# Seven block products for the down projections of two FFN chunks, with x moved through three tiles and the low parts of weight blocks shared between VectorE and GpSimd

## The reference

```python
def swiglu(h, w_gu, w_d):
    gu = h @ w_gu
    g, u = gu[..., :D_FF], gu[..., D_FF:]
    return (jax.nn.silu(g) * u) @ w_d
...
hh = modulate(x, norm_g[l, 0], mod[:, 0], mod[:, 1])
x = x + 0.5 * mod[:, 2, None] * swiglu(hh, ffn_w_gu[l, 0], ffn_w_d[l, 0])
```

## Time and profile before

| what | value |
|---|---|
| median of 3 runs | 2325.98 us |
| the runs | 2325.94 to 2327.22 us |
| the profiled execution, own time | 2325.12 us |
| its span | 2323.3 us |
| granted TensorE clock | 0.99 of full |

### The profile page before, as it was taken

One profiled execution on the slowest core, in us unless ns is written; L12 is line 12 of the kernel. 1 busy time (PEld: TensorE's weight loads), 2 busy tenths in 40 slices (PEclk: granted clock), 3 DMA queues, 4 the chain that ended last, 5 costly groups with the idle time before them and its releaser, 6 DMA issues.

```text
span 2323.3 us, 42586 instructions
## 1 busy us (share of the span) xinstructions
PE 2229.3 (96%) x17538; PEld 2093.0 (90%) x17538; DVE 1505.5 (65%) x2615; ACT 1004.6 (43%) x1673; POOL 173.7 (7%) x133
## 2 busy tenths in 40 slices
PE   5999999999999999999999999999799899999998
PEld 4999999999999999999999999999544499999997
DVE  5585748587657766666457757667466555858585
ACT  4342424367453434345353424345344534434252
POOL 0100101000000101010000101010000101001010
PEclk9999999999999999999999999999899999999999
DMA  7334334512423434333533333335699641322222
GB/s 321 128 127 164 123 114 152 180 42 100 148 91 117 161 123 143 138 128 111 210 126 112 125 128 123 123 107 211 215 361 407 233 146 50 104 102 82 83 94 74
DMA packets 77234, 338.41 MB, mean 146 GB/s; under 512 B 9458, under 2 KB 13682, under 8 KB 60914
## 3 DMA queue, kind: packets, MB, share of 16 engines
q1 hardware_dynamic: 73810, 330.83, 39.9%
q10 hardware_dynamic: 3232, 4.87, 0.6%
HBM read 328.44 MB, written 7.23 MB: 144 GB/s over the span
## 4 chain that ended last, share of the span: by engine, by line
PE 84%; DVE 8%; ACT 4%; issue 2%; DMA 1%; POOL 0%; SPq 0%; ACTq 0%; DVEq 0%; POOLq 0%
PE ps L616 21%; PE ps L697 12%; PE ps L700 12%; PE ps L699 11%; PE ps L618 11%; PE ps L626 3%; PE ps L628 3%; PE ps L627 3%; PE ps L586 2%; DVE w_lo L1694 1%; PE ps L942 1%; DMA ada_pro<-in_ada_w 1%; PE ps L974 1%; DVE xc L2131 1%; PE ps L961 1%
## 5 line engine op out<-in xcount | busy, mean ns | idle before, releaser
L697 PE MATMUL ps<-bx,w_hi 128*128 128x288 f32 x2016 | 597.1, 296 | 0.0
L700 PE MATMUL ps<-bx,w_lo 128*128 128x288 f32 x2016 | 595.2, 295 | 0.0
L699 PE MATMUL ps<-bx,w_hi 128*128 128x288 f32 x2016 | 593.9, 295 | 0.0
L616 PE MATMUL ps<-hn_hi,w_hi 128*128 128x288 f32 x1360 | 381.5, 295 | 2.6 <-POOL hn_lo L2380 2.3
L697 PEld LDWEIGHTS ps<-bx,w_hi 128*128 128x128 f32 x2016 | 378.5, 188 | 5.8 <-issue 5.3
L616 PE MATMUL ps<-hn_lo,w_hi 128*128 128x288 f32 x1360 | 380.1, 295 | 0.0
L700 PEld LDWEIGHTS ps<-bx,w_lo 128*128 128x128 f32 x2016 | 379.7, 188 | 0.0
L699 PEld LDWEIGHTS ps<-bx,w_hi 128*128 128x128 f32 x2016 | 379.7, 188 | 0.0
L618 PE MATMUL ps<-hn_hi,w_lo 128*128 128x288 f32 x1360 | 292.2, 296 | 0.0
L1694 DVE TENSOR_TENSOR w_lo<-raw,w_hi 128x1536 fp32r<-128x1536 f32 (+2 forms) x108 | 205.9, 1907 | 111.7 <-ACT w_hi L1061 93.7
L616 PEld LDWEIGHTS ps<-hn_hi,w_hi 128*128 128x128 f32 x1360 | 255.4, 188 | 7.4 <-issue 4.2
(11 more groups left out here) (293 smaller groups left out, 4084.6 us busy)
## 6 DMA issues: line engine op xcount, KB each, us to landing
raw<-in_w_gu SPq DMA_DIRECT2D x88, 1024.0 KB, 4.9
ada<-in_ada_w SPq DMA_DIRECT2D x120, 512.0 KB, 7.4
raw<-in_w_d SPq DMA_DIRECT2D x48, 768.0 KB, 4.2
kr<-in_k_cache SPq DMA_DIRECT2D x64, 512.0 KB, 7.1
vr<-in_v_cache SPq DMA_DIRECT2D x60, 512.0 KB, 12.1
ada_pro<-in_ada_w SPq DMA_DIRECT2D x8, 1024.0 KB, 18.4
raw<-in_w_d SPq DMA_DIRECT2D x16, 512.0 KB, 3.6
ada_early<-in_ada_w SPq DMA_DIRECT2D x16, 512.0 KB, 10.7
```

The lines of the kernel that those rows point to most:

```text
L616: pe.matmul(ps[:, 2 * s + n, 0:TH], whi, rhs(k, n)[r], start=(k == 0 and r == 0), stop=False)
L697: pe.matmul(out, whi[:, cols], high, start=(fresh and k == 0), stop=False, skip_group_check=not fresh)
L699: pe.matmul(out, whi[:, cols], low, start=False, stop=False, skip_group_check=not fresh)
L700: mm = pe.matmul(out, wlo[:, cols], high, start=False, stop=(k == 3), skip_group_check=not fresh)
```

## The change

The down stages of the second and third chunk become units of seven products too, of three tiles of depth: 7 x 3 x 3 = 63 matmuls. `seven_unit` replaces `fast_unit`, and the up and down units from the second chunk's first to the fourth chunk's last up unit form one chain. For this:

- **Turned tiles.** The up units of chunks two and three make, beside g * u, sums for t1, t2, t3 (in `tb`) and t4 (in `hn_hi`, `hn_lo`): VectorE does one sum of 288 columns a unit in product_first and two more in product_second of the last three; ScalarE makes high parts, VectorE the low parts of t2 and t4, GpSimd those of t1 and t3.
- **Low parts of weight blocks.** In up units on VectorE as before. For down units, GpSimd makes those of A11 (but not for the second down unit of a chunk), A22, A12 and S34, of 384 and 768 columns; VectorE makes S12. The order on each engine is written out below. GpSimd's low part of g * u has 288 columns in the first three up units and 576 in the last three.
- **x.** `tb` lies over x tiles 3 to 7 and the late constants. In the chain x has three places (`x_of`): ScalarE's queue stores tiles 3 to 7 to yT at its first unit; after each down unit it stores two tiles and fetches two. SyncE fetches the whole x and the late constants in the fourth chunk's up stage (`x_back`).
- **Results.** The residual of a down unit comes in three parts: row2 (second tile, after the unit), c11 and c12 (first tile, within it).
- The order and the waits of the constants' loads at the start are changed, and semaphores are merged.

The core of the diff:

```diff
+                if starts_chain(s):
+                    for i, v in enumerate(chain_of(s)):
+                        seven_unit(v, i == 0)
...
+                    for k in range(kh):
+                        high, low = seven_at(v, i, k)
...
+                if v["down"] == 0:
+                    pe.wait_ge(sems["turned_lo"], 2 * q + 1)
                 product(1, fresh=True).then_inc(sems["f_prod"], 1)
                 pe.wait_ge(sems["f_seed"], f + 1)
+                if v["down"] == 0:
+                    pe.wait_ge(sems["t_lo"], LOWS * s["ffn"] + 4 + 5 * (q % 2) + 3)
                 product(2).then_inc(sems["f_prod"], 1)
```

ScalarE, in the loop over the chain:

```diff
+                        if down == 0:
+                            turn_high("t2", "t2", 2, 1, SUMS * s["ffn"] + 12 * (q % 2) + 4 + 11)
+                        if before is not None and before["up"] is not None:
+                            fast_high(before)
...
+                        if after_down:
+                            x_store(before, 0)
...
+                        if i == 0:
+                            act.dma_start(yT[3:KT].rearrange("k p t -> p k t"), x[:, 3:KT, :]).then_inc(sems["x_out"], 16)
+                        if after_down:
+                            x_store(before, 1)
+                        if after:
                             high_a22(u + 1, f + 1, False)
                             high_s12(u + 1, f + 1, False)
+                        if turned is not None and up == 3:
+                            turn_high("t1", "t2", 0, 3, SUMS * s["ffn"] + 12 * (q % 2) + 4 + 3)
+                        if turned is not None and up == 5:
+                            turn_high("t2", "t2", 0, 2, SUMS * s["ffn"] + 12 * (q % 2) + 4 + 8)
+                            turn_high("t3", "t3", 0, 2, SUMS * s["ffn"] + 12 * (q % 2) + 4 + 8)
+                            turn_high("t4", "t4", 0, 2, SUMS * s["ffn"] + 12 * (q % 2) + 4 + 9)
```

VectorE:

```diff
+                    def residual_row2(v):
+
+                        st, k, u = v["s"], 2 * v["down"] + 1, v["u"]
+                        x_ready(v, 1)
+                        dve.wait_ge(sems["w_done"], u + 1 + CREDITS["w_done"])
+                        add_scaled(st, k, slice(0, TH), ps[:, 2 if u % 2 else 0, 0:TH])
+                        dve.wait_ge(sems["f_c22"], v["f"] + 1)
+                        add_scaled(st, k, slice(TH, SEQ), c22[:, 0:PB])
+                        dve.wait_ge(sems["s0_free"], u + 1 + CREDITS["s0_free"])
+                        add_samples(st, k, c22[:, PB:TH], st["res"], "s1_free")
...
+                        if before is not None and before["up"] is not None:
+                            product_first(before)
+                        if before is not None and before["down"] is not None:
+                            residual_row2(before)
...
+                        if up is not None:
+                            low_s34(u, f)
+                        if down == 0:
+                            turn_low("t2", 2, 1, HIGHS * s["ffn"] + 7 * (q % 2) + 4 + 5)
+                        if after:
                             sums_123(u + 1, f + 1)
...
+                            if not down:
+                                low_a11(u + 1, f + 1)
+                        if down == 0:
+                            turn_low("t3", 2, 1, HIGHS * s["ffn"] + 7 * (q % 2) + 4 + 6)
                         dve.wait_ge(sems["f_prod"], 5 * f + 3)
                         dve.wait_ge(sems["f_p5"], f + 1)
                         dve.tensor_tensor(ps[:, 3, 0:TH], ps[:, bank, 0:TH], p5, ALU.add).then_inc(sems["f_u4"], 1)
...
+                        if after and after["up"] is not None:
                             low_a22(u + 1, f + 1)
...
+                        if after:
+                            low_s12(u + 1, f + 1)
+                        if v["s"]["turned"] is not None and up == 5:
+                            turn_low("t2", 0, 2, HIGHS * s["ffn"] + 7 * (q % 2) + 4 + 2)
+                            turn_low("t4", 0, 2, HIGHS * s["ffn"] + 7 * (q % 2) + 4 + 4)
+                        if down == 0:
+                            turn_low("t4", 2, 1, HIGHS * s["ffn"] + 7 * (q % 2) + 4 + 7)
+                        if down is not None:
+                            residual_c11(v)
```

GpSimd:

```diff
+                        if down is not None:
+                            low_s34(u, f)
+                        if before is not None and before["up"] is not None:
+                            product_low(before)
...
+                        if after and down:
+                            low_quarter("a11", 0, 0, 0, u + 1, f + 1)
...
+                        if after and after["down"] is not None:
+                            low_quarter("a22", 6, 1, 1, u + 1, f + 1)
+                        if turned is not None and up == 3:
+                            turn_low("t1", "t2", 0, 3, HIGHS * s["ffn"] + 7 * (q % 2) + 4 + 1)
+                        if turned is not None and up == 5:
+                            turn_low("t3", "t3", 0, 2, HIGHS * s["ffn"] + 7 * (q % 2) + 4 + 3)
+                        if after and after["down"] is not None:
+                            low_quarter("a12", 3, 0, 1, u + 1, f + 1)
```

More of the change, by code:

```diff
@@ L145, in ffn @@
         for c, tiles in enumerate(CHUNKS):
-            stage("fast" if c else "up", tiles, src=w_gu[2 * layer + which], row=first)
+            stage("fast" if c else "up", tiles, src=w_gu[2 * layer + which], row=first,
+                  turned=c - 1 if c in (1, 2) else None)
             count["h"] += tiles
             count["fast"] += tiles if c else 0
+            count["ups"] += tiles if c else 0
             first += tiles
@@ L180, in trunk, with chain_of, starts_chain @@
             width[s["u"] + m] = 256 * s.get("k", KT)
-    fast_of = {s["u"] + m: s["fast"] + m for s in plan if s["kind"] == "fast" for m in range(s["units"])}
+    sevens = [s for s in plan if s["kind"] == "fast" or s.get("seven")]
+    fast_of = {s["u"] + m: s["fast"] + m for s in sevens for m in range(s["units"])}
+    half_tiles = {s["u"] + m: 4 if s["kind"] == "fast" else 3 for s in sevens for m in range(s["units"])}
+    def chain_of(s):
+        units = []
+        for t in plan[plan.index(s):]:
+            if t not in sevens:
+                break
+            for m in range(t["units"]):
+                up = t["kind"] == "fast"
+                units.append({"u": t["u"] + m, "f": t["fast"] + m, "up": m if up else None,
+                              "down": None if up else m, "s": t})
+        return units
+    def starts_chain(s):
+        return s["kind"] == "fast" and s["row"] == CHUNKS[0]
     u_out = next(s["u"] + s["units"] for s in plan if s["kind"] == "rglru")
@@ L884, in _ @@
                                  freed="hq_free" if s["kind"] == "q" and m == s["units"] - 1 else None)
-                if s["kind"] == "fast":
-                    for m in range(s["units"]):
-                        fast_unit(u0 + m, s["fast"] + m, m == 0)
-                if s["kind"] == "down":
+                if starts_chain(s):
+                    for i, v in enumerate(chain_of(s)):
+                        seven_unit(v, i == 0)
+                if s["kind"] == "down" and not s.get("seven"):
                     h_all = s["h"]
@@ L1327, in _ @@
                     high_s34(u0, s["fast"], True)
                     high_a22(u0, s["fast"], True)
-                    for m in range(s["units"]):
-                        u, f, more = u0 + m, s["fast"] + m, m + 1 < s["units"]
-                        bank = 2 if u % 2 else 0
-                        if m:
-                            fast_high(m - 1)
+                    for i, v in enumerate(chain):
+                        u, f, up, down = v["u"], v["f"], v["up"], v["down"]
+                        before, after = chain[i - 1] if i else None, chain[i + 1] if i + 1 < len(chain) else None
+                        turned = v["s"]["turned"]
+                        q = 2 * s["ffn"] + (turned or 0)
+                        bank = 2 if u % 2 else 0
+                        after_down = before is not None and before["down"] is not None
+                        if down == 0:
+                            turn_high("t2", "t2", 2, 1, SUMS * s["ffn"] + 12 * (q % 2) + 4 + 11)
+                        if before is not None and before["up"] is not None:
+                            fast_high(before)
@@ L1353, in _ @@
                             split_unit(((u + 1) // 2, u + 1), 0)
+                        if after_down:
+                            done = 8 * before["s"]["turned"] + 2 * before["down"] + 2
+                            for n in (done + 1, done + 2):
+                                if n < 16:
+                                    x_load(s["ffn"], n, done)
                         act.wait_ge(sems["out0_full"], u + 1)
[L1355 to L1356 removed]
+                        if up is not None:
+                            act.activation(gate2, ps[:, 3, 0:TH], ACT.Silu).then_inc(sems["s0_free"], 1)
```

(17 more changed lines are left out.)

387 lines of the change are left out of this document (277 added, 110 removed).

## The result

The changed kernel takes 2450.45 us (2444.94 to 2453.78, 4 runs), the kernel before 2325.96: 1.0532 times as long, 95% interval 1.0509 to 1.0554. I had said 2367 and a range up to 2392: the direction was right, the size a third of what came, and the time lies outside the range.

What follows compares the result with a forecast made beforehand. TensorE's order of work bounds the kernel before; the shared GpSimd/VectorE port would delay the changed units. Unit delays 51.6, cover -12.2 and x 2 sum to +41.4 on 2325.1: 2366.5, rounded to 2367 us, range 2306 to 2392.

Steps and rivals of the forecast that it cites:

- The bound of the kernel before, and the prices: Whole kernel: TensorE sets the time, 0.3 us slack before the fifth product; GpSimd's 384 columns priced at 1.01 us.
- What the change removes: 32 down units: 288 matmuls, 38.2 us off TensorE; a unit can then take 8.35 us at least.
- The down unit, 10.0: Later down units: GpSimd's low parts hold up VectorE, fifth product 1.66 us late, 10.0 us against 9.5.
- the rival in which such steps are held: Rival: VectorE's PSUM steps are held too, or the x store is late; 2390 to 2400, chance 0.06.
- a median near 1.4 for the sums of 384 columns: Sign in the down units' VectorE sums: median near 1.4 us instead of 0.55.
- Part cover: Rival: one low part misses the sums, 0.9 off each of 24 units; 2345 to 2326, chances 0.09 slower, 0.07 near 2326.
- The first down unit, 11.4 and the fifth up unit, +0.8: Each chunk: first down unit 11.4 us against 9.5 (+1.9); fifth up unit's fifth product 0.8 us late.
- The sixth up unit: Each chunk's last up unit: A22, t3, A12 on GpSimd, t2, t4 on VectorE; +2.25 us.
- The up units, "+0" for the first four: Up units one to four: an added VectorE sum offset by GpSimd's smaller low part, +0 us.
- x through three places, 2 us: Five-tile x store 0.5 us late per FFN, 2 in all; fetched x tiles land in units before their use.
- Cover, -12.2: Modulation parts on TensorE ahead of eight units let VectorE's work get on: 12.2 us saved.
- the rival with full cover: Rival: GpSimd's work is wholly covered; pure 2287, 2303 with half of some delays left; full or nearly full cover, chance 0.20.

Runs made afterwards that it cites:

- the doubled low part: Kernel before the change, with GpSimd making each product's low part twice in the fast units: 2386.84 us, ratio 1.0264.
- 2387.22: Changed kernel with product_second moved back behind low A12 and sum_4 in the up units: 2387.22 us, ratio 1.0262.
- 2391.02: Kernel before the change, with only product_second moved ahead of low A12 and sum_4: 2391.02 us, ratio 1.0274.
- 2417.77: Changed kernel without the stores and loads of x inside the chain (part of x wrong): 2417.77 us, ratio 1.0398.
- 2352.76: Changed kernel with product_second back and x in transit left out (part of x wrong): 2352.76 us, ratio 1.0111.
- 2377.39: Changed kernel with product_second back and the down units' low parts on VectorE: 2377.39 us, ratio 1.0218.
- 2321.84: Changed kernel with product_second back, down units' low parts on VectorE, x in transit left out (part of x wrong): 2321.84 us, ratio 0.9982.

## Why the prediction was wrong

**The bound of the kernel before, and the prices.** Right. TensorE set the time, and the slack before the fifth product was as small as read: the doubled low part, 1.1 us more on VectorE, made a unit 0.92 longer, so 0.2 of the 0.3 was there. GpSimd's 384 columns, where nothing holds them, take 1.00 to 1.01, as the slope had it.

**What the change removes.** Right in size, 38 us of matmuls. A down unit came to 8.35 only where a modulation part stood ahead of it, as the third one of the first FFN in the changed kernel. Even with x out and VectorE doing all of it, the down units of the fourth FFN take 8.75, 8.5 and 9.6 and the first 10.3.

**The down unit, 10.0.** Right in length, 9.86 and 9.78, but not by the port alone. The timeline of the second down unit of the changed kernel, VectorE, GpSimd, ScalarE; its first product starts at 2175.39:

```profile
2176.03 1.58 DVE L2222 SCALAR_TENSOR_TENSOR x<-sg,mod_g,x 128x224 f32<-128x224 f32 x1
...
2178.51 1.25 DVE L1865 TENSOR_TENSOR scratch<-scratch,raw 128x384 f32<-128x384 f32 x1
2179.68 1.37 DVE L1866 TENSOR_TENSOR raw<-raw 128x384 f32<-128x384 f32 x1
2180.98 0.45 DVE L2292 TENSOR_TENSOR ps<-ps,sg 128x288 f32<-128x288 f32 x1
```
```profile
2175.48 1.87 POOL L2672 TENSOR_TENSOR w_lo<-raw,w_hi 128x768 fp32r<-128x768 f32 x1 [2.58 <-ACT w_hi L1191]
2177.91 2.74 POOL L2665 TENSOR_TENSOR w_lo<-raw,w_hi 128x384 fp32r<-128x384 f32 x2 [0.55 <-ACT w_hi L1167]
```
```profile
2176.80 0.34 ACTq L1428 DMA_DIRECT2D out_yT<-x  x1
2177.24 0.53 ACT L1167 ACTIVATE w_hi<-raw 128x384 fp32r<-128x384 f32 x1
```

The residual's second step was stopped by low S34 (1.58 instead of 0.44), two of three sums by low A11 and A22 (1.25 and 1.37 instead of 0.55). The add ended 6.04 after the unit's first product began, where I had 6.4; TensorE stood 1.25 before the fifth product, where I had 1.66. The residual's first step, which reads PSUM, took its 0.52, so the rival in which such steps are held (the third of the four, not the last) is out. That is the lock that the Trainium skill describes (SBUF — State Buffer, "SBUF: two separate sides"), and here too the trace agrees with it, on both sides: which operations stop and that they stop for the whole of the other.

I had said a median near 1.4 for the sums of 384 columns. In the changed kernel the medians of the three are 1.59, 1.26 and 0.55, and 50 of the 96 sums were stopped; with product_second back and x out it is 28 of 96, and most take 0.55. The down units there show why the port alone is cheaper: second and third ones with no modulation part beside them took 9.1 to 9.4 in eight of twelve cases and 9.8 to 10.0 in four. That is the rival *Part cover*. In the units compared here a store of x tips it. Its issue on ScalarE (L1428) stands ahead of the high part of A11 (L1167), which starts 0.45 behind the seed instead of 0.30; low A11 on GpSimd starts 2.52 after the first product instead of 2.36. Then it misses the residual's last step, and it and low A22 fall among the sums. The prediction's "the two stores and two loads of x a unit lie in gaps of over 1 us" did not hold there. This is read from the timelines and was not tried by itself, and the four long units have no store, so other small delays do the same. That the down units came near 10.0 in the changed kernel is in part luck: with product_second back and no x, the three later down units of a chunk of the fourth FFN cost nothing in sum, where I had 1.5.

**The first down unit, 11.4 and the fifth up unit, +0.8.** Near enough once the order is back: 11.15 and 11.92 (11.80 and 13.32 in the changed kernel). The sixth up unit was over-priced, +2.25 against +1.8.

**The up units, "+0" for the first four and nothing for the fourth chunk.** This is the first step that failed. I priced what was added and left the moved product_second out. It is worth 63 us, shown from both sides (2387.22 and 2391.02), and 65 with x out (2417.77 less 2352.76).

**x through three places, 2 us.** The second step that failed: "the x tiles fetched ... land in units before their use" was written with no row behind it. A tile's place is free when its store has landed, 4.4 us in the median, and the load takes 3.1 more, and longer beside 2 MB of modulation weights; a down unit takes 9.9. It is worth 33 to 34 us with GpSimd's low parts, and 56 with faster down units (2377.39 less 2321.84). The other term here, 2 us for the store of five tiles, was nothing: the first up units of the second chunks are as long as before once the order is back.

**Cover, -12.2.** Right, but hidden in the changed kernel, where the chains of the four FFNs are 30.5, 30.7, 27.9 and 28.4 us longer than before: those with modulation parts lost as much as the fourth. With product_second back and x out they are 4.0, 5.3, 4.1 and 8.6 longer, so the three FFNs with parts lost 12.4 less than three like the fourth would have. The parts cover VectorE's work, but the weights that come for them made x late; moving those loads gave 16 us.

Put together, in the order in which they were taken away: 2450.45, less 63.2 (order), less 34.5 (x), less 30.9 (low parts on GpSimd) is 2321.84. The last two overlap, as 9 and 10 us for the low parts with x in transit show, so how the 65 us are shared between them depends on the order. The steps that I did price, all of them in the kernel of 2352.76, gave 26.5 us over the kernel before, where the sum had 39.4: that overestimate hid a part of what was left out. From 2321.84 to the 2287 of the rival with full cover, 35 us are left: by the unit lengths it is in the main what VectorE still adds in the first and last down and the fifth and sixth up units. That was read, not tried.

## What to carry to other kernels

Go through the new order of every engine against the old, line by line, and price what has moved before what is new: one step that waits, put ahead of two that don't, cost 63 us, as much as all the rest of the change (61). A tile whose place is freed by a store needs store and load in sequence before its use; that sum belongs beside the shortest stage it will run in, with the largest other load beside it. And when one of two late things is cured, measure the other again: the same edit was worth 9, 16 or 31 us by what else was late.

## What the runs showed of the hardware

GpSimd's two-input operation and VectorE's with two SBUF inputs took turns, one for one, where both had work queued: in the doubled low part GpSimd got its second turn after one VectorE operation, though three sums stood in line, in 48 units of 48. A low part of 128 x 768 on GpSimd took 1.87 and one of 128 x 384 1.00, by the slope that I had taken from 288 and 576 columns (1.85 and 1.01). Where a store of x was issued on ScalarE's queue, the next ScalarE operation started 0.15 later; GpSimd's operations then fell among VectorE's sums, and the down unit took 9.9 instead of 9.2. A store of 288 KB took 4.4 us to land (median) and a load 3.1, where a store of 1,440 KB took 5.5: a small store cost four fifths of one five times as large.
